# Memory key and value blocks placed between the second-half w_o blocks, their weight splits in pairs, and the memory queries two heads ahead

## The reference

```python
mixed = concat([rms_norm(fox_o, g_fox_out), rms_norm(mla_o, g_mla_out)])
x = x + mixed @ w_o
mem_k, mem_v = rms_norm(mem, g_mem_src) @ w_mk, rms_norm(mem, g_mem_src) @ w_mv
q = rms_norm(x, g_mem) @ w_mq
p = softmax(einsum("bqhd,bmhd->bhqm", q, mem_k) * 128 ** -0.5)
x = x + einsum("bhqm,bmhd->bqhd", p, mem_v) @ w_mo
hf = rms_norm(x, g_ffn)
x = x + (silu(hf @ w_gate) * (hf @ w_up)) @ w_down
y = rms_norm(x, g_final)
```

## Time and profile before

| | us |
|---|---|
| median of 3 runs (989.58 to 992.02) | 990.03 |
| the profiled execution | 990.94 |
| its span in the trace | 989.1 |

### The profile page before, as it was taken

How to read it: one execution, slowest core, us unless ns; L and a number is a source line. 1 busy time by engine, 2 the same in 40 slices (tenths; PEclk the granted TensorE clock), 3 DMA queues, 4 the chain that set the end, 5 groups by cost and what they waited for, 6 DMA issues and landing times.

```text
span 989.1 us, 15581 instructions
## 1 busy us (share of the span) xinstructions
PE 898.1 (91%) x6186; PEld 853.7 (86%) x6186; DVE 387.9 (39%) x615; ACT 382.7 (39%) x686; POOL 402.4 (41%) x209
## 2 busy tenths in 40 slices
PE   6999997989998986696689999999999998999995
PEld 6978986778887876686679899999999998999994
DVE  6354555556677725523436322222222221121113
ACT  6343555656777222334335332233332232121210
POOL 5456943434225324771106533333333332433320
PEclk9999998889999997798759999999999999999997
DMA  7334312001024221141102232222222222222302
GB/s 221 107 95 141 97 58 67 1 17 44 2 95 151 65 85 43 46 130 39 43 1 82 72 101 73 79 84 85 85 85 85 85 79 60 80 81 78 99 17 96
DMA packets 25092, 75.46 MB, mean 76 GB/s; under 512 B 2880, under 2 KB 5000, under 8 KB 24904
## 3 DMA queue, kind: packets, MB, share of 16 engines
q1 hardware_dynamic: 25040, 74.74, 24.7%
HBM read 68.20 MB, written 6.53 MB: 76 GB/s over the span
## 4 chain that ended last, share of the span: by engine, by line
PE 75%; POOL 7%; issue 6%; DVE 6%; ACT 4%; DMA 1%; DVEq 0%; SPq 0%; ACTq 0%; POOLq 0%
PE ps L369 23%; PE ps L370 22%; PE ps L371 22%; POOL wlo L1642 3%; PE ps L532 2%; PE ps L515 1%; POOL sqacc L1797 1%; PE ps L541 1%; PE ps L387 1%; ACT whi L858 1%; DVE small L1382 1%; DVE mql L1552 1%; POOL sqacc L1760 1%; POOL vhl L1647 1%; PE ps L395 1%
## 5 line engine op out<-in xcount | busy, mean ns | idle before, releaser
L369 PE MATMUL ps<-hhi,whi 128*128 128x288 f32 x1120 | 342.1, 305 | 37.8 <-POOL wlo L1642 18.4
L370 PE MATMUL ps<-hhi,wlo 128*128 128x288 f32 x1120 | 338.8, 302 | 0.0
L371 PE MATMUL ps<-hlo,whi 128*128 128x288 f32 x1120 | 337.9, 302 | 0.0
L1786 POOL TENSOR_TENSOR wlo<-wraw,whi 128x1024 fp32r<-128x1024 f32 (+1 forms) x68 | 160.2, 2357 | 255.2 <-ACT whi L858 255.2
L369 PEld LDWEIGHTS ps<-hhi,whi 128*128 128x128 f32 x1120 | 219.2, 196 | 40.4 <-POOL wlo L1642 27.0
L370 PEld LDWEIGHTS ps<-hhi,wlo 128*128 128x128 f32 x1120 | 217.7, 194 | 0.0
L371 PEld LDWEIGHTS ps<-hlo,whi 128*128 128x128 f32 x1120 | 217.5, 194 | 0.0
L1642 POOL TENSOR_TENSOR wlo<-wraw,whi 128x1024 fp32r<-128x1024 f32 (+1 forms) x49 | 118.0, 2412 | 220.8 <-ACT whi L858 220.5
L858 ACT ACTIVATE whi<-wraw 128x1024 fp32r<-128x1024 f32 (+1 forms) x117 | 119.4, 1023 | 136.8 <-PE ps L371 121.7
L369 PE MATMUL ps<-hidhi,whi 128*128 128x288 f32 x352 | 104.8, 298 | 3.4 <-DVE hidlo L1617 3.4
L370 PE MATMUL ps<-hidhi,wlo 128*128 128x288 f32 x352 | 104.8, 298 | 0.0
(11 more groups left out here) (239 smaller groups left out, 1493.9 us busy)
## 6 DMA issues: line engine op xcount, KB each, us to landing
wraw<-w_ff SPq DMA_DIRECT2D x44, 512.0 KB, 3.5
wraw<-w_front SPq DMA_DIRECT2D x41, 512.0 KB, 3.6
wraw<-w_down SPq DMA_DIRECT2D x16, 512.0 KB, 3.6
wraw<-w_front SPq DMA_DIRECT2D x8, 384.0 KB, 3.2
wraw<-w_down SPq DMA_DIRECT2D x8, 384.0 KB, 3.2
xs<-x_t SPq DMA_DIRECT2D x8, 288.0 KB, 5.7
xa<-x_t SPq DMA_DIRECT2D x8, 288.0 KB, 4.7
out_y<-xb SPq DMA_DIRECT2D x8, 288.0 KB, 2.3
```

What stands on the lines that cost most here:

```text
L369: nc.tensor.matmul(out, lh, rh, start=start, stop=False)
L370: nc.tensor.matmul(out, ll, rh, start=False, stop=False)
L371: return nc.tensor.matmul(out, lh, rl, start=False, stop=stop)
L1786: g.tensor_tensor(ffw(c, 1, 1, n)[:, 0, :], wraw[:, c % 2, 0:n], f(ffw(c, 0, 1, n)[:, 0, :]), ALU.subtract)\
```

## The change

1. **Block order.** Key, value and query blocks are dealt in between the `w_o` blocks: 25 wof, 26 wof, 27 mk, 28 wof, 29 mk, 30 wof, 31 mk, 32 wom, 33 mk, 34 wom, 35 mv, 36 wom, 37 mv, 38 wom, 39 mv, 40 mq, 41 mv, 42 to 44 mq, 45 to 48 mo (wof, wom: first and second half of `w_o`).
2. **PE.** `memory_keys(0)`, `(1)`, `(2)` stand in ticks 84, 90, 94, the memory norm's `columns` and `spread` in ticks 86, 89, and the mla norm's `columns` in tick 92. Then `mixed(0)`, `mixed(1)`, `memory_keys(3)`, three times two `mixed` and one `memory_values`, `query(0)`, `columns`, `memory_values(3)`, `spread`, `query(1)`. In the cross-attention only `query(2)` (steps 0 to 3) and `query(3)` (steps 5 to 8) are left, and the first `mspread` comes a step later.
3. **ACT.** Splits stand in pairs behind odd tiles (35, 36 behind m = 1; 37, 38 behind 3; 39, 40 behind 5); 31 and 32 stand at ticks 91, 92.
4. **Sums of squares.** The 14 additions into `sqacc` around `mixed` and `memout` go from POOL to DVE (`square_sum`).
5. **Divisors.** `S_RI` has two buffers, so DVE's reciprocals wait for the `rb` before last; POOL builds `rb` first in its tick.

The number of instructions is the same on PE, ACT and SP; 14 TENSOR_TENSOR go from POOL to DVE.

```diff
+            def memory_keys(m):
+                b = B_MK[m]
+                pe.wait_ge(f_lo, b + 1)
+                for k in range(KT):
+                    mm = product(ps[:, m, 0:NM], [front(b, lo, KT, 128)[:, k, :] for lo in (0, 1)],
+                                 [t[:, k, :] for t in (memh, meml)], k == 0, k == KT - 1)
+                mm.then_inc(f_used[b % 3], 1)
...
+                if s == 84:
+                    pe.wait_ge(s_mmlo, 8)
+                    pe.wait_ge(s_ex, TICKS)
+                    memory_keys(0)
...
             mixed(0)
-            pe.wait_ge(n_rc, 3)
-            spread(rows2(6), small[:, S_RCC:S_RCC + 5], range(TT)).then_inc(n_row, 1)
-            for m in range(1, 8):
-                mixed(m)
+            mixed(1)
+            memory_keys(3)
+            for c in range(3):
+                mixed(2 * c + 2)
+                mixed(2 * c + 3)
+                memory_values(c)
...
-            pe.wait_ge(s_wmt, 5)
+            pe.wait_ge(s_wmt, 7)
             query(0, 0, 8, lambda k: pe.wait_ge(r_lo, k + 1))
...
+            pe.wait_ge(r_acc, 7)
+            columns(2, sqacc).then_inc(n_col, 1)
+            memory_values(3)
+            pe.wait_ge(n_rc, 4)
+            spread(rows2(2), small[:, S_RCC:S_RCC + 5], range(TT)).then_inc(n_row, 1)
+            pe.wait_ge(s_wmt, 8)
+            query(1, 0, 8)
...
-                h, u = s // 5, s % 5
-                if h < 3 and u < 3:
-                    if u == 0:
-                        pe.wait_ge(s_mqev, h + 1)
-                        if h > 1:
-                            pe.wait_ge(m_rbs, h - 1)
-                    query(h + 1, 3 * u, min(3 * u + 3, 8))
+                if s in (0, 5):
+                    pe.wait_ge(s_mvev, 2)
+                    need(pe, s_mqev, s // 5 + 2)
+                if s < 10 and s % 5 < 4:
+                    query(2 + s // 5, 2 * (s % 5), 2 * (s % 5) + 2)
...
+            def square_sum(m, at, count):
+                dve.wait_ge(r_sq, at + m + 1)
+                need(dve, r_acc, count + m - 1)
+                v.tensor_tensor(sqacc[:, 0:T], sqacc[:, 0:T], tmp2[:, m % 2, :], ALU.add).then_inc(r_acc, 1)
...
-                    need(dve, s_rb, p)
+                    need(dve, s_rb, p - 1)
```

More of the change, by code:

```diff
@@ L636, in _ @@
                     turn(s - 2)
[L639 to L650, removed]
+                if s == 84:
+                    pe.wait_ge(s_mmlo, 8)
+                    pe.wait_ge(s_ex, TICKS)
+                    memory_keys(0)
+                elif s == 86:
                     pe.wait_ge(s_mmacc, 3)
@@ L693, in query @@
                         c = slice(half * HT, half * HT + HT)
-                        mm = product(ps[:, 4 + half, 0:HT], [front(b, lo, KT, 128)[:, k, :] for lo in (0, 1)],
+                        mm = product(ps[:, 2 * PAIR_MQ[m] + half, 0:HT], [front(b, lo, KT, 128)[:, k, :] for lo in (0, 1)],
                                      [t[:, k, c] for t in x1], k == 0, k == 7)
@@ L1492, in _ @@
                     v.reciprocal(small[:, S_RCC:S_RCC + 5], small[:, S_COL:S_COL + 5]).then_inc(s_frc, 1)
+                if s == 88:
+                    dve.wait_ge(n_sd, 2)
+                    v.reciprocal(small[:, S_MRC:S_MRC + 2], small[:, S_MCOL:S_MCOL + 2]).then_inc(n_rc, 1)
+                if s == 90:
+                    dve.wait_ge(n_row, 2)
+                    v.tensor_copy(rmem[:, :], ps[:, 5, 0:NM]).then_inc(n_rs, 1)
+                if s in (91, 92):
+                    dve.wait_ge(n_rs, 2)
+                    memory_key(s - 91)
+                if s == 94:
+                    dve.wait_ge(n_sd, 3)
+                    v.reciprocal(small[:, S_RCC:S_RCC + 5], small[:, S_COL:S_COL + 5]).then_inc(n_rc, 1)
                 if 75 <= s < 83:
@@ L1552, in query_lo @@
                 v.tensor_tensor(mql[:, h, :], mqf[:, h, :], f(mqh[:, h, :]), ALU.subtract).then_inc(s_mqlo, 1)
-            query(0)
-            query_lo(0)
+            for h in range(2):
+                query(h)
+                query_lo(h)
             for s in range(5 * MH + 6):
@@ L1744, in _ @@
                         g.tensor_tensor(msq[:, 0:n, :], msq[:, 0:n, :], msq[:, n:2 * n, :], ALU.add).then_inc(s_mmacc, 1)
-            for b in (31, 32, 33):
-                rest(b)
             def memory_key_lo(m):
@@ L1780, in _ @@
             memory_value_lo(1, 3)
-            for b in range(44, 48):
+            for b in range(44, 49):
                 rest(b)
@@ L1787, in remainder @@
                     .then_inc(g_lo, 1)
[L1789 to L1798 removed]
+            for c in range(4):
+                remainder(c)
             with pool.Fori(0, FT // 2) as i:
@@ L1919, in _ @@
             load(28)
-            load(29)
             sp.wait_ge(s_qk, 5 * 2 * H)
@@ L2021, in pairs @@
         return [np.concatenate([by_rows(w[:, 128 * m:128 * m + 128]) for m in (2 * b, 2 * b + 1)], 1) for b in range(4)]
-    parts += pairs(w_o[0:512])
-    parts += [by_rows(w_mk[:, 128 * m:128 * m + 128]) for m in range(MH)]
-    parts += pairs(w_o[512:1024])
+    wof, wom = pairs(w_o[0:512]), pairs(w_o[512:1024])
+    mk = [by_rows(w_mk[:, 128 * m:128 * m + 128]) for m in range(MH)]
+    mv = [by_rows(w_mv[256 * b:256 * b + 256]) for b in range(4)]
     mq = [by_rows(w_mq[:, 128 * m:128 * m + 128]) for m in range(MH)]
-    parts += mq[0:1]
-    parts += [by_rows(w_mv[256 * b:256 * b + 256]) for b in range(4)]
-    parts += mq[1:4]
+    parts += [wof[0], wof[1], mk[0], wof[2], mk[1], wof[3], mk[2], wom[0], mk[3], wom[1], mv[0], wom[2], mv[1], wom[3], mv[2],
+              mq[0], mv[3], mq[1], mq[2], mq[3]]
     parts += pairs(w_mo)
```

265 lines of the change are left out of this document (133 added, 132 removed).

## The result

The changed kernel takes 945.16 us in the median of four runs (942.73 to 946.38), the kernel before 990.5. The ratio is 0.954, with a 95% interval of 0.9521 to 0.956: faster, by 45 us. The prediction was 952 in a range of 938 to 974. The profiled execution of the changed kernel took 946.38 us, with a span of 944.6, so 44.5 us went from the span of 989.1.

What follows compares the result with a forecast made beforehand. PE was bound by a chain of waits for late weights and query remainders, not by a busy engine. Gains 3 + 6.5 + 10.4 + 18.4 = 38.3 us off the 989.1 us span gave 950.8, median some 952, range 938 to 974.

Steps and rivals of the forecast that it cites:

- Tick 20: PE's 2.78 us wait for `rb` at tick 20: building `rb` first gains 3 us, bounds 0 and 6.
- Keys among the ticks: Key blocks dealt among the ticks: weights ready, the 3.73 us gap and its slow clock go; gain 6.5 us, bounds 3.7 and 8.
- To the first scores: From `mixed(1)` to the first scores: 67.4 us falls to 56.5 to 57; gain 10.4, bounds 46.5 and 66 us.
- the key eviction: Ahead of `mixed(2)`: PE waits 0.6 us for the eviction of the fourth key block.
- Nine such steps at 2.0 us: DVE before `query(0)`: nine instructions in turns with POOL end 17 us behind the last tile, giving 8 us of waits.
- Cross-attention: First scores to `memout`: 75.5 us falls to 57.1 without `query(1)` and three gaps; gain 18.4, bounds 10 and 24.
- head 2 goes from covered to uncovered: Cross-attention: head 2 has no query to fill PE, 5.5 us more than its work without the query.
- `memout` and the first feed-forward tile: From `memout` to the first feed-forward tile: row-sum gain and late remainder cancel; 0 us, bounds +1.5 and -2.
- A: Before the first scores: turns of DVE and POOL cost nothing PE sees; 10 us more gain, 942 us; chance 0.17.
- B: PE never returns to the fast clock; values, `query(1)`, first two heads run half at 1.2 GHz; 968 us; chance 0.20.
- C: Among the `w_o` tiles: split pairs late too, three gaps with their clock, some 14 us, stay; 966 us; chance 0.07.
- D: Slower than before: DVE becomes the bound of both stages, needing over 9.3 us for two tiles; 996 us; chance 0.04.

Runs made afterwards that it cites:

- the lumps: query(2) and query(3) each done in one piece at steps 0 and 5, not two parts a step, against the changed kernel: 949.44 us, ratio 0.9573.
- The kernel with the fewest gaps: Changed kernel with ACT and DVE reordered behind the last tiles and POOL waiting for DVE's remainders and sums: 936.18 us, ratio 0.9446.

## Why the prediction held, and where it was off

**What bounds the kernel: right.** Late weights and late query remainders, not an engine, made both slow stretches. Making the splits late again brings 15 us back, making the remainders late brings back 4.9 us of the cross-attention in the profile and 3.5 us of the median. That the rest of the old gaps ended by `mql` (12.5 us in all) has the same cause is read from the profiles alone.

**The sum: 38.3 us forecast, 44.5 measured.** Two stretches gave 5.0 and 4.0 us more than forecast. Of that, 2.2 was hidden by tick 20, which gave less, and 1.5 by small losses at the end; 1.0 came from scatter ahead of the change. So the median is closer to the forecast than the terms are.

**Tick 20: mis-sized.** 3 us forecast, 0.8 measured, and no measurable gain alone. The step that failed is "I take 3 us, with DVE's reciprocal no longer behind it and the clock staying up". The wait shrank by 1.76 us and not by 2.78, and the clock did not stay up: it was 0.50 behind the wait in both kernels and rose later in the code of the changed one, with 2.90 us for 17 matmuls that took 1.90. The lower bound's reason, the next wait just behind, was not what took the gain. Why the clock rose later stays open; it is no accident of one execution, since the last 38 matmuls up to the end of this stretch ran at 0.85 and 0.84 in the two profiles of the changed kernel, and at 1.00 before.

**Keys among the ticks: right.** 6.5 forecast, 6.4 measured.

**To the first scores: mechanism right, size too small.** 10.4 forecast, 15.4 measured. Waits were put at 8 us inside `query(0)` and measured 3.9, the clock at 2.5 and measured 1.7 (0.13 x 12.7); the key eviction, put at 0.6, took 0.61. The step that failed is "Nine such steps at 2.0 us put the last remainder 17 us behind the last tile": the last tile ends at 387.6, the last remainder at 400.2, 12.6 us behind it. The price of 2.0 came from a place where POOL was at work without a break. Two engines in turns need, together, nearly the sum of their work: the two sums and POOL's pair, 1.61 and 4.70 us with the engines apart, took 5.8 us side by side. But here POOL had only six instructions in 17.5 us. DVE's eight with both inputs in SBUF took 2.95 and 1.07 for one, 2.70 for two and 5.13 for four, by whether a POOL instruction was in progress. I had the right count for both engines two sentences earlier and then priced DVE as if each of its instructions met one of POOL's.

**Cross-attention: mechanism right, size too small.** 18.4 forecast, 22.4 measured; 0.25 of that is the old stretch, which took 75.75 us and not the 75.5 of the prediction. From the scores of one head to those of the next it was 15.4, 18.7, 20.6 and 21.1 us with the tail; it is 9.5, 12.8, 12.0 and 19.0. The step that failed is "head 2 goes from covered to uncovered, which I put at 5.5 us more": by my terms it would take 20.6 - 6.4 - 3.8 - 2.5 + 5.5 = 13.4 us and took 12.0, and covering two heads is worth 2.1 us in all (the lumps). The last head, which was to stay at clock 0.50, ran at 0.82 and gave 2.1 us. With a gap of 1.61 us put back ahead of it, the same code ran at 0.51; but the lumps and the changed order on DVE, which have no such gap, had 0.65 and 0.63, so the gap is not the whole of it, and part of the 2.1 us may be luck.

**`memout` and the first feed-forward tile: right.** 0 forecast, -0.7 measured, inside its bounds. On POOL the sums cost as much.

**The rule of the Trainium skill** ("SBUF — State Buffer", section "Who interferes with whom") was put against the change, and the runs bear it out: with the two engines kept apart the four remainders take 3.00 us instead of 5.13, and moving 14 additions from one to the other changed nothing, 946.6 against 945.77.

**The rivals.** A, in which the turns cost nothing that PE sees, gave 942, B 968, C 966, D 996. The result lies between the forecast and A, though not by A's mechanism: the remainders were not 0.8 us each, and the kernel that keeps the two engines apart is 9 us faster still. B did not occur: the clock was 0.87 through the values and `query(1)`, and 0.95 or better through heads 0 to 2. C did not occur either, but was close by: the first remainder of the third pair ended at 387.28 us and PE began with it at 387.45, where the prediction gave the pairs 1.5 to 3 us in hand, and one tile later the whole 15 us are back, near C's own 14. D needed DVE over 9.3 us for two tiles; it was busy 19.5 us of the 25.7 with the six tiles.

## What to carry to other kernels

When two engines take turns, moving work from one to the other may gain nothing, as with the 14 additions here (946.6 against 945.77 us); what counts is who goes first. Let the one for which the bottleneck engine waits finish, and hold the other back by a semaphore as long as its own result isn't due: here three such waits, with a few instructions moved on ACT, DVE and POOL, gave 9 us on top of the 45. Price a turn by how many instructions of the other engine fall into the stretch, not by the slowest example in the trace. And a gap of the matmul engine costs itself plus what the clock takes behind it, here up to as much again (8.3 us of gaps and some 8.4 through the clock), so a small edit that makes a prefetch late by one tile can take back a third of what a reordering won.

## What was not expected of the hardware

The clock behind a gap is not a fixed price, even for identical code. In the 20 us or so of the last head the granted clock was 0.82 in the changed kernel, and 0.87, 0.65, 0.63 and 0.51 in variants that were edited only ahead of it; the stretch took 19.0 us, and 17.8, 21.4, 20.4 and 20.8. Around `memout` it was 0.96 in the changed kernel, and 0.91 and 0.85 in two variants with no edit there, for 46.1, 48.0 and 51.1 us. That is probably a good part of the 4 to 9 us between runs of one kernel, since the slow runs have the lower mean clock: of the six with DVE's order changed, the fastest took 940.7 us at 0.972 and the slowest 949.81 at 0.959. The kernel with the fewest gaps had runs within 2 us (935.39 to 937.41). What decides it in a given execution stays open.
